# A diffusion backbone with experts: the router reads the raw rows, and its place among TensorE's work changes

## The reference

```python
def rmsnorm(x, g):
    y = xf * lax.rsqrt(jnp.mean(xf * xf, axis=-1, keepdims=True) + EPS)
    return (y * g).astype(x.dtype)

def channel_mixer(x, l, shift, scale, gate):
    h = rmsnorm(x, norm_ffn_g[l]) * (1 + scale) + shift
    return x + gate * hierarchical_moe(h, router_grp[l], router_exp[l], moe_w1[l], moe_w3[l], moe_w2[l])

def hierarchical_moe(h, w_grp, w_exp, w1, w3, w2):
    g_prob = jax.nn.softmax(t @ w_grp); g_idx = jnp.argmax(g_prob)        # the best of 4 groups
    e_logits = einsum('td,gde->tge', t, w_exp) of that group
    top_v, top_i = lax.top_k(e_logits, 2)                                   # the best two of its 4 experts
    gate = softmax(top_v) * g_prob of the group, at the two experts
    y = sum over experts of (silu(t @ w1) * (t @ w3) * gate) @ w2
```

## Time and profile before

| | |
|---|---|
| median of 3 runs | 800.33 us (796.5 to 801.96) |
| the profiled execution | 797.47 us |
| its span, first to last instruction | 795.6 us |
| TensorE products / weight loads busy | 750.4 / 419.5 us |
| VectorE (DVE) / ScalarE (ACT) / POOL busy | 234.0 / 165.0 / 50.3 us |
| moved by DMA | 289.66 MB, 364 GB/s over the span |
| mean granted TensorE clock | 0.970 of full |

### The profile page before, as it was taken

One profiled execution on the slowest core, in us unless ns is written; L12 is line 12 of the kernel. 1 busy time (PEld: TensorE's weight loads), 2 busy tenths in 40 slices (PEclk: granted clock), 3 DMA queues, 4 the chain that ended last, 5 costly groups with the idle time before them and its releaser, 6 DMA issues.

```text
span 795.6 us, 10420 instructions
## 1 busy us (share of the span) xinstructions
PE 750.4 (94%) x4039; PEld 419.5 (53%) x4039; DVE 234.0 (29%) x665; ACT 165.0 (21%) x372; POOL 50.3 (6%) x74
## 2 busy tenths in 40 slices
PE   4699989989999999999999999999999899999996
PEld 4388458754344444434478866875333434333444
DVE  2300441541112111111489943153212111211215
ACT  3120240340000100010330874252011001010003
POOL 5014000010000000000100000000110000101100
PEclk9889999989999999999999999988999899999997
DMA  8998999979999999999998259667999996999971
GB/s 301 400 396 349 390 409 428 366 281 402 429 425 426 428 427 425 425 428 421 399 401 341 88 213 377 256 234 300 423 430 428 420 424 258 394 429 422 416 298 56
DMA packets 43506, 289.66 MB, mean 364 GB/s; under 512 B 4513, under 2 KB 5997, under 8 KB 30386
## 3 DMA queue, kind: packets, MB, share of 16 engines
q1 hardware_dynamic: 37616, 275.78, 84.7%
q0 software_dynamic: 5056, 11.98, 4.0%
q10 hardware_dynamic: 770, 1.06, 0.4%
HBM read 285.63 MB, written 8.52 MB: 370 GB/s over the span
## 4 chain that ended last, share of the span: by engine, by line
PE 82%; DMA 7%; DVE 4%; issue 2%; ACT 2%; POOL 1%; SPq 1%; PEld 0%; DVEq 0%; PEldq 0%; POOLq 0%
PE ps L539 79%; DMA ring<-in_conv_w 4%; DMA ring<-in_w_in_ab 3%; DVE work L1962 1%; PE ps L769 1%; PE ps L842 1%; SPq L476 1%; PE ps L810 0%; DVE rstd L1699 0%; PE ps L1121 0%; ACT work L1354 0%; POOL work L1580 0%; ACT work L1350 0%; DVE back L2213 0%; PE ps L1241 0%
## 5 line engine op out<-in xcount | busy, mean ns | idle before, releaser
L539 PE MATMUL ps<-ring,work 128*64 128x512 f32 x1088 | 304.1, 595 | 1.1 <-issue 0.5
L539 PEld LDWEIGHTS ps<-ring,work 128*64 128x64 f32 x1088 | 93.9, 137 | 143.8 <-issue 143.2
L539 PE MATMUL ps<-back,ring 128*128 128x256 f32 x656 | 147.9, 386 | 5.2 <-ACT back L1314 1.9
L539 PEld LDWEIGHTS ps<-back,ring 128*128 128x128 f32 x656 | 125.2, 193 | 27.0 <-issue 4.2
L539 PE MATMUL ps<-bench,work 128*64 128x512 f32 x208 | 93.2, 596 | 0.1
L539 PE MATMUL ps<-spare,work 128*64 128x512 f32 x176 | 77.6, 594 | 0.0
L539 PE MATMUL ps<-back,work 128*64 128x512 f32 x160 | 72.0, 596 | 0.0
L1962 DVE TENSOR_TENSOR work<-work,ps 128x256 f32<-128x256 f32 x34 | 19.4, 613 | 142.3 <-PE ps L539 142.1
L2177 DVE SCALAR_TENSOR_TENSOR work<-work,dw 128x256 f32<-128x256 f32 x120 | 50.8, 478 | 1.0
L1380 ACT ACTIVATE work<-ps 128x512 f32<-128x512 f32 x15 | 9.0, 597 | 178.9 <-PE ps L539 178.9
L539 PE MATMUL ps<-ring,csil 128*32 128x512 f32 x336 | 40.9, 615 | 3.2 <-DMA ring<-in_w_ada 3.2
(11 more groups left out here) (249 smaller groups left out, 647.1 us busy)
## 6 DMA issues: line engine op xcount, KB each, us to landing
ring<-in_moe_w SPq DMA_DIRECT2D x60, 2048.0 KB, 18.8
ring<-in_w_ada SPq DMA_DIRECT2D x21, 2048.0 KB, 16.9
bench<-in_moe_w SPq DMA_DIRECT2D x11, 2048.0 KB, 17.9
spare<-in_moe_w SPq DMA_DIRECT2D x10, 2048.0 KB, 20.2
back<-in_moe_w SPq DMA_DIRECT2D x9, 2048.0 KB, 18.4
ring<-in_conv_w SPq DMA_DIRECT2D x6, 2048.0 KB, 24.9
ring<-in_moe_w SPq DMA_DIRECT2D x6, 1024.0 KB, 29.7
ring<-in_w_in_ab SPq DMA_DIRECT2D x2, 2048.0 KB, 26.0
```

Source lines behind the costliest of these rows:

```text
L539: return nc.tensor.matmul(out, lhsT, rhs, start=start, stop=stop, skip_group_check=True)
```

## The change

The router's sums are formed from xT in place of hT. With 1/root the reciprocal of a token's RMS root, a sum is (1/root) * sum over channels of x * (gain * w), plus the sum over channels of shift * w. DVE weighs the router's weights with shift and gain (weigh_route). TensorE does the products right behind the row sums, adds one product with ones for the shift's sum and two that turn the roots onto token partitions, and only then the modulation rows. DVE combines sums, root and shift at the head of route. Norm weight and scale move from DVE to ACT's scale operand (norm_moe: one DVE product a chunk). Transposes go chunk by chunk and follow the modulation rows; the turning of the modulation part stands behind the rank products. ACT copies the banks in the order 0, 2, 1, 3.

```diff
+            def logits(l, start, stop):
+                pe.wait_ge(wg_ready, l + 1)
+                for k in range(start, stop):
+                    if k == 0:
+                        mm(ps_shift, ones[:, :], wshift[:, :, :])
+                    for g in range(2):
+                        mm(ps_logit[:, g, :], xT[:, k, g * TG:(g + 1) * TG], wg[:, k, g, :], False, k == DC - 1)
...
             def moe(l, n):
+                logits(l, 0, DC)
+                pe.wait_ge(root_ready, n + 1)
+                for g in range(2):
+                    last = mm(ps_root[:, g:g + 1], root[0:1, g * TG:(g + 1) * TG], ones[0:1, 0:1], False, True)
+                last.then_inc(route_done, 1)
                 pe.wait_ge(mod_taken, (4, 8)[l])
                 for j in range(len(ADA_ROOT[l])):
                     ada_rows(ADA_ROOT[l], j)
                 for k in range(DC):
                     pe.wait_ge(h_ready, DC * n + k + 1)
                     for g in range(2):
-                        last = mm(ps_logit[:, g, 0:20], hT[:, k, g * TG:(g + 1) * TG],
-                                  wr[:, l, k, :], k == 0, k == DC - 1)
-                last.then_inc(route_done, 1)
-                ada_turn(ADA_ROOT[l])
-
-                for g in range(2):
-                    for k in range(DC):
                         last = nc.tensor.transpose(ps[:, 2 * g + k // 4, (k % 4) * P:(k % 4 + 1) * P],
                                                    hT[:, k, g * TG:(g + 1) * TG], ident)
...
                 mm(ps_rank[:, 2, :], ones[:, :], mask[:, 1, :], False, True).then_inc(rank_done, 1)
+                ada_turn(ADA_ROOT[l])
                 pe.wait_ge(htok_ready, 4 * l + 4)
...
@@ norm_act, on ACT
-                                                    ACT.Identity, bias=mod[:, shift[0], shift[1] + k, g:g + 1])
+                                                    ACT.Identity, bias=mod[:, shift[0], shift[1] + k, g:g + 1],
+                                                    scale=gain[:, shift[0], 1, k, g:g + 1] if n % 2 else 1.0)
@@ moe_act, on ACT: both loops over the banks
-                for b in range(4):
-                    act.wait_ge(htok_done, 4 * l + b + 1)
+                for n, b in enumerate((0, 2, 1, 3)):
+                    act.wait_ge(htok_done, 4 * l + n + 1)
@@ fetch_rows, on POOL
-                    pool.wait_ge(htok_ready, 4 * l + 2 * g + 2)
+                    pool.wait_ge(htok_ready, 4 * l + g + 3)
@@ on DVE
+            def weigh_route(l):
+                shape = [P, DC, 2, 20]
+                w = wr[:, l].unsqueeze(2).to_broadcast(shape)
+                link(V.tensor_tensor(wg[:, :, :, :], w, mod[:, l, 24:32, :].unsqueeze(3).to_broadcast(shape), ALU.mult))
+                link(V.tensor_reduce(wshift[:, :, :], wg[:, :, :, :].rearrange("p k g e -> p g e k"), AX.X, ALU.add))
+                V.tensor_tensor(wg[:, :, :, :], w, gain[:, l, 1].unsqueeze(3).to_broadcast(shape), ALU.mult).then_inc(wg_ready, 1)
+
+            def norm_moe(n):
+                norm_root(n)
+                for k in range(DC):
+                    V.tensor_tensor(hT[:, k, :], xT[:, k, :], rstd[:, :], ALU.mult).then_inc(hpre_ready, 1)
...
+            weigh_route(0)
             residual(1, psx, 0, 2, lambda k: product(dve, y_done[0], "out", 0, k))
-            norm_dve(1, lambda k, g: gain[:, 0, 1, k, g:g + 1])
+            norm_moe(1)
...
             def route(l):
                 dve.wait_ge(route_done, l + 1)
-                link(V.tensor_copy(lg[:, :, :], ps_logit[:, :, 0:20]))
+                V.tensor_copy(wshift[:, :, :], ps_shift)
+                link(V.reciprocal(rtok[:, :], ps_root))
+                for g in range(2):
+                    last = V.scalar_tensor_tensor(out=lg[:, g, :], in0=ps_logit[:, g, :], scalar=rtok[:, g:g + 1],
+                                                  in1=wshift[:, g, :], op0=ALU.mult, op1=ALU.add)
+                link(last)
...
             take_mod(1, 2, 4)
+            weigh_route(1)
             residual(3, sq, 1, 2, lambda k: dve.wait_ge(yb_ready, k + 1))
-            norm_dve(3, lambda k, g: gain[:, 1, 1, k, g:g + 1])
+            norm_moe(3)
```

More of the change, by code:

```diff
@@ L168, in backbone @@
         ps_rank = ps[:, 5, NT + 64:NT + 112].rearrange("p (s e) -> p s e", s=3)
-        ps_logit = ps[:, 4:6, NT:NT + 32]
+        ps_logit = ps[:, 4, NT:NT + 40].rearrange("p (g e) -> p g e", g=2)
+        ps_shift = ps[:, 4, NT + 40:NT + 80].rearrange("p (g e) -> p g e", g=2)
+        ps_root = ps[:, 4, NT + 80:NT + 82]
         ring = sb("ring", [P, SLOTS, DC * TW])
@@ L262, in backbone @@
         lg = sb("lg", [P, 2, 20])
+        wg = sb("wg", [P, DC, 2, 20])
+        wshift = sb("wshift", [P, 2, 20])
+        rtok = sb("rtok", [P, 2])
         r1 = sb("r1", [P, 2, 16])
@@ L356, in backbone @@
         route_done = sem("route_done")
+        wg_ready = sem("wg_ready")
         gexp_in = sem("gexp_in")
@@ L1477, in moe_act @@
                                          ACT.Copy).then_inc(htok_ready, 1)
-                for b in range(4):
-                    act.wait_ge(htok_ready, 4 * l + b + 1)
+                for n, b in enumerate((0, 2, 1, 3)):
+                    act.wait_ge(htok_ready, 4 * l + n + 1)
                     last = nc.scalar.activation(ps[:, b, :], cst[:, 0:512], ACT.Copy, scale=0.0)
```

## The result

The changed kernel is slower: a median of 806.98 us in 4 runs (804.75 to 812.17) against 799.7 us in 4 runs of the kernel before, a ratio of 1.0126 [1.0091, 1.0162]. Its profiled execution took 804.75 us with a span of 802.9 us, 7.3 more than before. An execution more than 1.5% above the fastest of its kernel is left out of the ratios: one of e5's (810.89 us, the one profiled, of which the order of the steps is read) and one of e8's (2679.38 us).

What follows compares the result with a forecast made beforehand. It took TensorE to bound the kernel (82% of the span), waiting for the router. Routing wins of 5.9 us without a clock fall and 2.5 with one gave a middle of 4.2, hence 795 us, range 790 to 801.

Steps and rivals of the forecast that it cites:

- the queues: On DMA: later weight tiles fit idle time, and POOL's row stores move at most 1.2 us earlier, with nobody waiting.
- the late tile's 5 us: On SP's queue: the tile replacing the modulation rows' first half leaves at 155.3, not 150.3, harmlessly in idle DMA time.
- rival 2: Ahead of the convolution: a longer weight wait eats layer 0's gain, leaving layer 1's 1.9 to 3.6, or 2.8 us; 14%.
- The routing stages: Row sums to first expert product: at full clock, layer 0 wins 2.3 us and layer 1 wins 3.6; 4.2 taken for both.
- 5.9 with no fall of the clock: Both routing stages: the total win in us if TensorE stays at full clock; 2.5 with a fall in both layers.
- The clock: TensorE likely falls to half clock as modulation rows begin, at 153 to 154 and 526 to 527, costing 1.7 us.
- two terms that I set too high: In layer 0's routing: router products at 5.0 us, and modulation rows' end to token copies' end, 157.2 to 160.8.
- my layer 0 with a fall: Layer 0's routing wins 0.6 us if half clock makes the modulation rows lose 1.7 us.
- my sum without a fall: Both routing stages at full clock: a total win of 5.9 us.
- Rival 1: TensorE in routing: clock falls during router products and stays half until the experts, making it 9 us slower; 6%.
- Rival 3: In routing: half-clock router products take up to 10 us, VectorE and token copies start no earlier; 0 to 1 us won; 12%.
- The weighing at nothing: On VectorE: weighing the router's weights takes 1.0 to 2.1 us, hidden in idle time of 19.47 and 3.87 us.

Runs made afterwards that it cites:

- e5: The kernel before, with the modulation rows' replacement tile sent late and the first store waiting for the third token copy: 803.3 us, 1.0066.
- e8: The changed kernel with modulation rows ahead of router products and the old order of transposes, copies and stores: 798.73 us, 1.002.
- e6: The changed kernel with the modulation rows ahead of the router products again: 797.84 us, 1.0001 against the kernel before.
- e2: The kernel before, with the tile replacing the modulation rows' first half held until six chunks of hT are ready: 797.79 us, 1.0013.
- e4: The changed kernel with the bank order and the store's wait of the kernel before: 808.06 us, 1.0154 against the kernel before.
- e10: The changed kernel with the back tile held until the token-row stores land (e1's kernel, timed again): 792.92 us in 12 runs, 0.9966.
- e9: The changed kernel with the released bench tile held until the first fetch of token rows has landed: 799.43 us, 1.0025.
- e1: The changed kernel with the back tile, and all tiles behind it, held until the token-row stores have landed: 792.96 us, 0.9969.
- e7: The kernel before with the back tile held until the token-row stores have landed: 797.48 us, 1.0013.
- e3: The kernel before with the first store waiting for the third token copy in place of the second: 805.68 us, 1.0134.

## Why the prediction was wrong

**The step that failed** stands under the queues: "POOL's row stores wait for the same copies and move at most 1.2 us earlier; nobody waits for them in the first pair." The second pair waits for them, by way of the fetch, 14 us into the first pair's products: 7.2 us in layer 0 and 6.3 in layer 1. I followed the stores to the first expert product and no further. The step just ahead of it, that the late tile's 5 us "fall into an idle stretch that remains, and restart moves with the expert products", is half right: the bench tile left 8.1 us behind the first expert product before and after (178.89 - 170.78, 175.52 - 167.41). But the idle stretch did not remain: ahead of the bench tile DMA was 0.42 busy before and is 0.89 after, in the windows above. It was the stretch in which the fetch had left, at 175.37. The late tile went out 4.6 us later (155.14 against 150.51), and the win itself brought the far end, the bench tile, 3.4 us forward. No rival held this: rival 2, loss to DMA, had the place and the direction wrong, as the wait ahead of the convolution vanished instead of growing.

**The routing stages** came out better than the sum: 2.2 and 3.8 against 4.2 taken for both, and 5.9 with no fall of the clock. The clock did fall where I said, as the modulation rows began: the granted clock was 1.00 in 147.3 to 151.5, 0.59 in 151.5 to 152.5 and 0.50 from there to 155. The modulation rows took 5.36 us in layer 0 against 3.68, 1.7 lost as forecast, at 0.68 over the stretch. What made up for it were two terms that I set too high. From the end of the row sums to the modulation rows took 4.2 us (147.35 to 151.51), not 5.0: the 32 records of 128x20 took 3.73, 0.117 each, against my 0.13. And the four token copies follow each other at 0.52 us: from the modulation rows' end (156.87) to the copies' end (159.89) took 3.0 us, not 3.6. Together these give 1.4 us back, most of what separates 0.6, my layer 0 with a fall, from 2.2. That the total, 6.0, came out at my sum without a fall, 5.9, is luck: the clock did fall, and terms set too high made up for it. Behind them the terms held: from the copies' end to the gates' first step 3.8 us (159.89 to 163.65) against 3.9, then 3.8 to the expert product, which waits for the modulation's last step as forecast.

**Rival 1** (half clock until the experts) did not come: transposes ran at 1.00 in 156.8 to 158.8 (the gather's first half, in 161.3 to 164.5, stood at 0.60, but the gate chain still ended 0.2 us behind the gather). The clock had come back ahead of them, under the modulation rows (0.50 in 154 to 155, 1.00 in 155.5 to 156.8), so this does not show whether it returns under transposes. The earlier trace rows are split on that: 1.00 behind the transposes of layer 0 (161.2 to 164.4), 0.50 through those of layer 1 (530 to 535).

**Rival 3** is what e6 shows for the half of the change without the new order: no routing time won. **The weighing at nothing** held: VectorE's idle time ahead of the residual shrank from 19.47 us to 17.74 in layer 0 and from 3.87 to 1.91 in layer 1, where the residual began 4.06 us behind the step before the weighing (L1703), as far behind that step as in the kernel before (L1688).

**The parts of the loss.** In layer 0 the fetch left 6.5 us later behind the first expert product than before (11.1 against 4.6) and took 6.5 us longer; less 5.8 us of slack (14.4 less 8.6), 7.2 us of wait are left. Against e6, at stores that stand alike, the faster routing brings the release forward by 2.75 us and the fetch leaves 2.5 us later; that the tile behind the modulation rows is what delays it there is argued, not shown. Neither that tile alone (e2) nor the store's wait alone (e4) decides. In the kernels without a hold it is whether the fetch gets through ahead of the released tile.

What stays open is why e10's median is only 0.34%, 2.7 us, lower, when its two routing stages win 2.2 and 3.5. The profiled execution, at 791.02 us, does show a win of that size, 6.4 us of span. It is one of seven of the twelve that lie at 790.7 to 793.0; the other five lie at 795.6 to 799.0, and no trace shows what those lose.

## What to carry to other kernels

When a stage becomes faster, list the small transfers that are issued in it and are needed a stage later, and ask which bulk transfers the faster stage releases: a margin of a few microseconds between the two is a cost waiting to appear (here a lead of 3.5 and 4.3 us that turned into a lag of 3.0 and 2.9). The idle stretch of DMA ahead of the bench tile (0.42 busy before, 0.89 after) was the one in which the fetch passed in 4.0 us, so look up the users of such a stretch before spending it. Where a small transfer must pass, order the bulk behind it. What counts is that it lands in time: e9 let the fetch go alone (4.3 and 3.4 us), e10 let it leave 10 us sooner (and take 11.3 and 10.2). One added wait on the bulk queue, e10's, turned 1.26% slower into 0.34% faster here.

## What the runs showed of the hardware

The first 512 KB store on POOL's queue took 2.9 to 4.8 us when the back tile left 0.9 us or more behind it (before, e2, e8) or was held until both stores had landed (e1, e7, e10). It took 8.9 to 12.5 us when that tile left within 0.7 us of it (the changed kernel, e3's layer 1, e4 to e6, e9; but 3.8 in e3's layer 0, at 0.6). The second store then lands 14.9 to 17.4 us after issue. The DMA view of the kernel after, from 160 to 177.7 us, holds just the two stores on q0 (1.05 MB) beside the weights on q1 (packets, MB, share of 16 engines):

```profile
q1 hardware_dynamic: 369, 5.26, 77.5%
q0 software_dynamic: 288, 1.05, 14.5%
```

The queue of the stores moved 288 packets while that of the weights moved 369, but a packet of the stores is 3.6 KB (1.05 MB by 288) and one of the weights 14.3 KB, so the stores got 17% of the bytes. During the fetch of layer 0 it is 144 packets (0.31 MB) to 240 (3.44 MB). How the two queues share an engine beyond these counts, no run shows.
